# Two dense tiles' gates: one-hot products against additions in memory by indirect transfers

## The reference, cut to what matters

```python
def peer(xn, w_q, sub_keys, u, v):
    q = (xt @ w_q).reshape(t, PEER_HEADS, 2, PEER_HALF)
    sc = jnp.einsum("thpc,hpnc->thpn", q, sub_keys)
    top_s, top_i = lax.top_k(sc, PEER_TOPK)              # 16 of 128, for each half
    cand_s = ...; cand_i = ...                           # 256 pairs of a head
    best_s, best_pos = lax.top_k(cand_s, PEER_TOPK)      # 16 of them
    idx = jnp.take_along_axis(cand_i, best_pos, axis=-1) # expert = 128 * left + right
    gate = jax.nn.softmax(best_s, axis=-1)
    # for each token: sum over its 8 * 16 slots
    hid = gelu(x . u[idx]) * gate
    out = sum(hid * v[idx])
```

## Time and profile before

| | before |
|---|---|
| median of 3 runs | 2321.95 us |
| the profiled execution: span | 2321.5 us |
| PE busy | 2190.6 us (94%) |
| DVE busy | 1544.2 us (67%) |
| ACT busy | 864.4 us (37%) |
| POOL busy | 438.8 us (19%) |
| memory read and written | 404.6 and 44.8 MB |

### The profile page before, as it was taken

The page is one execution under the profiler, slowest core; times in us unless marked ns, Lnnn a source line. Parts: engine busy times, 40 slices in busy tenths (PEclk is TensorE's granted clock), DMA queues, the critical chain, the costliest instruction groups (busy, mean ns, idle before and its releaser), DMA issues. The chain is left out here.

```text
span 2321.5 us, 29188 instructions
## 1 busy us (share of the span) xinstructions
PE 2190.6 (94%) x11110; PEld 1895.1 (82%) x11110; DVE 1544.2 (67%) x2711; ACT 864.4 (37%) x1431; POOL 438.8 (19%) x307
## 2 busy tenths in 40 slices
PE   7999899899999899898999999999998999988898
PEld 6777788688999889888788888999996798876577
DVE  4545434325999989864888888688887624447734
ACT  3345323322334644863333333333334432222322
POOL 0100000000122010001434335266661000004200
PEclk9999999899999999999999999999998999998999
DMA  5321133211678674678999999799992322310220
GB/s 213 111 87 55 50 142 132 95 37 60 227 251 258 184 245 156 195 233 284 358 384 385 383 384 367 255 356 358 357 335 108 146 85 93 107 55 1 109 100 37
DMA packets 211836, 451.35 MB, mean 194 GB/s; under 512 B 13808, under 2 KB 133616, under 8 KB 204912
## 3 DMA queue, kind: packets, MB, share of 16 engines
q1 hardware_dynamic: 174832, 315.24, 39.7%
q0 software_dynamic: 36864, 134.23, 15.9%
HBM read 404.60 MB, written 44.83 MB: 194 GB/s over the span
## 5 line engine op out<-in xcount | busy, mean ns | idle before, releaser
L1604 PE MATMUL bank<-Vh,Hh 128*128 128x512 f32 x768 | 299.7, 390 | 4.7 <-DVE Hl L1687 4.6
L1606 PE MATMUL bank<-Vh,Hl 128*128 128x512 f32 x768 | 300.3, 391 | 0.0
L1605 PE MATMUL bank<-Vl,Hh 128*128 128x512 f32 x768 | 300.1, 391 | 0.0
L1626 ACT ACTIVATE Vh<-Vr 128x1024 fp32r<-128x1024 f32 x128 | 135.8, 1061 | 302.4 <-PE bank L1606 296.6
L934 PE MATMUL bank<-XH,Ue 128*128 128x384 f32 x672 | 232.2, 346 | 13.8 <-DVE Ue L923 13.8
L972 POOL DMA_INDIRECT ring<-in_v,gidx x128 | 205.8, 1608 | 164.7 <-DVE x_res L984 69.1
L935 PE MATMUL bank<-XL,Ue 128*128 128x384 f32 x672 | 227.3, 338 | 0.0
L936 PE MATMUL bank<-XH,Ue 128*128 128x384 f32 x672 | 227.2, 338 | 0.0
L1682 DVE TENSOR_TENSOR Vl<-Vr,Vh 128x1024 fp32r<-128x1024 f32 x128 | 156.3, 1221 | 49.6 <-ACT Vh L1626 46.7
L972 POOL DMA_INDIRECT ring<-in_u_rows,gidx x92 | 114.8, 1248 | 381.6 <-DVE ghid L977 206.2
L1604 PEld LDWEIGHTS bank<-Vh,Hh 128*128 128x128 f32 x768 | 144.6, 188 | 35.6 <-DVE Hl L1687 6.4
(11 more groups left out here) (386 smaller groups left out, 4935.3 us busy)
## 6 DMA issues: line engine op xcount, KB each, us to landing
Vr<-in_v SPq DMA_DIRECT2D x128, 512.0 KB
ur<-in_u SPq DMA_DIRECT2D x86, 512.0 KB
W<-in_w_stream SPq DMA_DIRECT2D x19, 2048.0 KB, 8.2
Gr<-gates SPq DMA_DIRECT2D x32, 768.0 KB
XT<-in_u SPq DMA_DIRECT2D x42, 512.0 KB
early<-ar SPq DMA_DIRECT2D x84, 192.0 KB
A<-early SPq DMA_DIRECT2D x84, 192.0 KB
xs<-in_w_mixer SPq DMA_DIRECT2D x14, 1024.0 KB
```

What stands on the lines that cost most here:

```text
L1604: pe.matmul(ps, Hh[r][:, tok], Vh[r][:, cut], start=p == 0, stop=False)
L1605: pe.matmul(ps, Hh[r][:, tok], Vl[r][:, cut], start=False, stop=False)
L1606: mm = pe.matmul(ps, Hl[r][:, tok], Vh[r][:, cut], start=False, stop=p == PK - 1)
L1626: act.activation(Vh[q % RV][:], Vr[q % RR][:], ACT.Copy).then_inc(v_hi, 1)
```

## The change

- `phase_merge`: GpSimd clears a tile `zeros` [128, 512], and SP stores it over the first two dense tiles' part of the table in memory (`Scattered.clear`: eight stores of 2 MB, ahead of the phase's other loads); SP waits for them at the phase's end.
- `phase_table`: after `choose(1)` and `choose(2)` DVE computes each slot's place in the table (six small instructions), and `gates` writes to `sca.gate`. For each of the two tiles and each of the 128 slots GpSimd issues one indirect DMA that adds the 128 tokens' gates, one element each, to their places in memory (`Scattered.put`). Every 16 slots (one head) it waits until all before have landed, since two heads can name the same place. GpSimd first issues 15 of the gathers; the other 15 stand at every fifth put.
- The slices, turns and stores of those two tiles go. The third tile's carry 8 early blocks. The order is choose 0, 1, 2, 3, 7 blocks (`E_MID`), slices, 26 blocks (`E_LAST`); `choose` has 14, 19, 19 and 19 blocks and 0, 10, 10 and 10 dots. 112 blocks are early, 16 late.
- `phase_experts`: SP also waits for the last puts before the first load of the table. Positions 0 to 7 and 120 to 127 are late.
- Some semaphores of the second layer are merged, to have enough.

```diff
-E_SCORE, E_SLICES, E_LAST = (14, 18, 18, 18), 4, 4
-EARLY = sum(E_SCORE) + DT * E_SLICES + E_LAST
+SCATTERED = 2
+E_SCORE, E_MID, E_SLICES, E_LAST = (14, 19, 19, 19), 7, 8, 26
+EARLY = sum(E_SCORE) + E_MID + (DT - SCATTERED) * E_SLICES + E_LAST
-DOTS = (0, 12, 12, 12)
+DOTS = (0, 10, 10, 10)
...
@@ phase_merge, SP and POOL
             sp.dma_start(gat.x[:], c.t["norm2"]).then_inc(c.const_in, 16)
+            sca.clear(sp, zeros)
...
+            sp.wait_ge(sca.zeroed, 16 * 4 * SCATTERED)
...
+            pool.memset(zeros[:], 0.0).then_inc(sca.cleared, 1)
             norm_rsqrt(pool, c, N_EXPERTS)
...
+class Scattered:
+    ZERO = 512
...
+    def clear(self, sp, zeros):
+        sp.wait_ge(self.cleared, 1)
+        for quarter in range(4 * SCATTERED):
+            flat = self.c.t["gates"][quarter].rearrange("a p b t -> (a p b t)").rearrange("(p r w) -> p r w", p=P, w=self.ZERO)
+            sp.dma_start(flat, zeros[:].unsqueeze(1).broadcast_to(list(flat.shape))).then_inc(self.zeroed, 16)
+
+    def put(self, pool, n, s):
+        if s == 0 and n == 0:
+            pool.wait_ge(self.zeroed, 16 * 4 * SCATTERED)
+        if s % TOPK == 0 and s > 0:
+            pool.wait_ge(self.landed[n], 16 * s)
+        cells = self.c.t["gates"].rearrange("q a p b (t o) -> (q a p b t) o", o=1)
+        at = bass.IndirectOffsetOnAxis(ap=self.place[:, n, s:s + 1], axis=0)
+        pool.indirect_dma_start(out=cells, out_offset=at, in_=self.gate[:, n, s:s + 1], in_offset=None,
+                                compute_op=ALU.add).then_inc(self.landed[n], 16)
+
+    def done(self, eng):
+        for n in range(SCATTERED):
+            eng.wait_ge(self.landed[n], 16 * SLOTS)
...
@@ phase_table, POOL
-            for s in range(DOTS_TABLE):
-                gat.fetch(pool, s)
+            dots = 0
+            while dots < DOTS[1] + RG:
+                gat.fetch(pool, dots)
+                dots += 1
+            for n in range(SCATTERED):
+                pool.wait_ge(chosen, n + 2)
+                for s in range(SLOTS):
+                    if s % BETWEEN == BETWEEN - 1 and dots < DOTS_TABLE:
+                        gat.fetch(pool, dots)
+                        dots += 1
+                    sca.put(pool, n, s)
...
@@ phase_table, PE
-            products(E0, E_SCORE[0] + E_SCORE[1] + LEAD)
-            turn(1)
-            products(E2 + LEAD, E_SCORE[2] - LEAD)
-            slices(0, EH0)
-            products(E3, E_SCORE[3])
-            slices(1, EH1)
-            slices(2, EH2)
+            products(E0, EM + LEAD)
+            turn(3)
+            products(EM + LEAD, E_MID - LEAD)
+            slices(2, EH[2])
             products(EL, E_LAST)
...
@@ phase_table, DVE, choose(n)
+                if n <= SCATTERED:
+                    row = float(PK * Q_TOK)
+                    link(dve.tensor_copy(part[:, 0], out3[:, 0]))
+                    link(one(1, part[:, 0], Q_BLK - 1, ALU.bitwise_and))
+                    dve.tensor_copy(abf[:, 1], part[:, 1])
+                    link(dve.tensor_scalar(abf[:, 0], out3[:, 0], row, c.tab[:, T_PLACE + tt:T_PLACE + tt + 1], ALU.mult, ALU.add))
+                    link(dve.scalar_tensor_tensor(out=abf[:, 0], in0=abf[:, 1], scalar=Q_TOK - row, in1=abf[:, 0], op0=ALU.mult, op1=ALU.add))
+                    link(dve.scalar_tensor_tensor(out=sca.place[:, n - 1], in0=out3[:, 1], scalar=float(Q_BLK * Q_TOK), in1=abf[:, 0],
+                                                  op0=ALU.mult, op1=ALU.add))
                 gates(n)
...
@@ phase_experts, SP
                     early.table_done(sp)
+                    sca.done(sp)
                     load_g(0)
```

More of the change, by code:

```diff
@@ L113 @@
 T_PICK = T_SIN + TT * DH
-NTAB = T_PICK + TT * SH
+T_PLACE = T_PICK + TT * SH
+NTAB = T_PLACE + SCATTERED
 R_GQK = 0
@@ L985, in add, with __init__ @@
                                  op0=ALU.mult, op1=ALU.add).then_inc(self.used, 1)
+class Scattered:
+    ZERO = 512
+    def __init__(self, c, ctx):
+        self.c = c
+        own = c.rows[:, R_GQK:R_GQK + 2 * SCATTERED * SLOTS].rearrange("p (f n s) -> p f n s", f=2, s=SLOTS)
+        self.place, self.gate = own[:, 0].bitcast(U32), own[:, 1]
+        self.cleared, self.zeroed = signals(c.nc, ctx, "sc_cleared sc_zeroed")
+        self.landed = signals(c.nc, ctx, " ".join(f"sc_landed{i}" for i in range(SCATTERED)))
+    def clear(self, sp, zeros):
[15 more added lines that the diff above has]
+            eng.wait_ge(self.landed[n], 16 * SLOTS)
 def phase_query(c, SC, early):
@@ L1086, in _, with phase_table @@
                         query_out(dve, dve.tensor_copy, g, qd)
-def phase_table(c, ijg, early, SC, gat):
+def phase_table(c, ijg, early, SC, gat, sca):
     nc, t = c.nc, c.t
@@ L1144, in phase_table @@
         E0, E1, E2 = 0, E_SCORE[0], E_SCORE[0] + E_SCORE[1]
[L1145 to L1149, removed]
+        E3 = E2 + E_SCORE[2]
+        EM = E3 + E_SCORE[3]
+        EH = [EM + E_MID + max(tt - SCATTERED, 0) * E_SLICES for tt in range(DT)]
+        EL = EH[DT - 1] + E_SLICES
+        J0 = SCATTERED * NSL
+        PER = E_SLICES // 4
         TICKS = [*[0.2] * NQ, *[0.52] * NQ, *[0.2] * NQ, *[0.28] * NQ, 0.43, 1.07, *[0.15] * PH, *[0.42] * PH, *[0.15] * PH, *[0.21] * PH,
@@ L1188, in stores @@
                 for i in range(4):
-                    early.load(sp, e + i + 3)
+                    turns(e + i * PER, PER - 1)
+                    early.load(sp, e + i * PER + PER + 2)
                     store(4 * tt + i)
[L1191 to L1197, removed]
+                    early.keep(sp, e + i * PER + PER - 1)
+            turns(E0, EM + E_MID)
+            for tt in range(SCATTERED, DT):
+                stores(tt, EH[tt])
             turns(EL, E_LAST)
@@ L1278, in slices @@
                     quarter = j // QSL
-                    if s % QSL == 0 and quarter >= 2:
-                        act.wait_ge(early.tabled[quarter % 2], 16 * PIECES * (quarter // 2))
+                    if s % QSL == 0 and quarter - 4 * SCATTERED >= 2:
+                        act.wait_ge(early.tabled[quarter % 2], 16 * PIECES * (quarter // 2 - 2 * SCATTERED))
                     if s + 1 < NSL:
@@ L1303, in _ @@
             scored(1, E1)
[L1304 to L1307, removed]
+            scored(2, E2)
             scored(3, E3)
-            slices(1, EH1)
-            slices(2, EH2)
+            gelus(EM, LEAD)
+            turned(3)
+            gelus(EM + LEAD, E_MID - LEAD)
+            slices(2, EH[2])
             gelus(EL, E_LAST)
@@ L1480, in _, with phase_experts @@
             choose(2, E2)
-            fill(0, EH0 + 1)
-            slices(0, EH0)
             choose(3, E3)
-            fill(0, EH1 + 1)
-            slices(1, EH1)
-            slices(2, EH2)
+            fill(0, EH[2] + 1)
+            slices(2, EH[2])
             fill(0, EARLY)
-def phase_experts(c, early, gat):
+def phase_experts(c, early, gat, sca):
     nc, t = c.nc, c.t
@@ L2544, in build @@
                 if upto >= 5:
-                    phase_table(c, ijg, early, SC, gat)
+                    phase_table(c, ijg, early, SC, gat, sca)
             if upto >= 6:
-                phase_experts(c, early, gat)
+                phase_experts(c, early, gat, sca)
         with ExitStack() as mix:
@@ L2585, in _tables @@
                     tab[(2 * (SG * cc + g) + x) * HG + h, T_PICK + (SG * cc + g) * HG + h] = 1.0
+    for tt in range(SCATTERED):
+        tok = tt * P + np.arange(P)
+        tab[:, T_PLACE + tt] = tok // Q_TOK * (PK * PK * Q_TOK) + tok % Q_TOK
     nf = DH // 4
```

67 lines of the change are left out of this document (35 added, 32 removed).

## The result

The changed kernel takes 2502.45 us, the median of 4 runs (2499.35 to 2505.7), beside 2323.05 us for the kernel before (4 runs, 2321.37 to 2325.95). The ratio is 1.0766, with a 95% interval of 1.0749 to 1.0784: 7.7% slower. The forecast was 2356 us in a range of 2275 to 2405, so the side was right and the size was not; the time lies next to the 2520 us of the rival "the add costs an extra descriptor".

A forecast was written before the change was run, and what follows sets the result against it. GpSimd's queue of puts was to bound the table stage and transfers the expert loop: +100.4 (table) - 68 (loop) + 2 (PE's clock) = +34, so 2321.95 + 34 = 2356 us, range 2275 to 2405.

The forecast's parts named there:

- the add costs an extra descriptor: Rival, table stage: two reads set up per element, 0.93 us more per put, end near 1315, about 2520 us; chance 0.11.
- The price of a put: GpSimd in the table stage: priced like an indirect gather, 0.94 us, 1.24 us from start to start undisturbed.
- The puts' surroundings: Table stage: first put at 699, 2.1 us each during slices, 3 us per wait for 16 landings, end at 1147.
- GpSimd keeps pace: Rival, table stage: puts at an undisturbed 1.24 us, end at 1083, 2290 us; break-even 1.38 us per put; chance 0.27.
- Cheaper puts: Rival, table stage: a 4-byte put needs less than a 4 KB gather, PE's 1072 ends the stage, 2279 us; chance 0.10.
- No ceiling: Rival, expert stage: slow puts, but DMA reaches 440 GB/s, loop 580 us, 104 less, 2320 us in all; chance 0.12.
- The 518 us: PE's part of the table stage: 466 for 112 blocks, 31 for slices, some 21 filling and stalls, to 1072 us.
- the sentence in brackets: Table stage: VectorE uses a dot each 8 us, five rows ahead; last dot up to 5 us late, cost nothing.
- 61 and 3 to enter: Third tile's slices with 8 blocks, bounded by PE: 61 us and 3 to enter, 64, of which 33 are blocks.
- Zeros: Eight 2.1 MB stores before `phase_merge`'s loads take 37 and 43 us; cost taken as nothing, range 0 to 18 us.
- The expert loop: Expert stage: transfers at 405 GB/s, 4.49 us per position, loop 618 us, 68 us less; between 104 and 49.
- The clock: PE after standing still before the expert stage: 2 us added for its clock.

The follow-up runs named there:

- e1_plain: The changed kernel with its 256 one-element puts as plain writes, without the addition: 2370.04 us.
- e2_back: The changed kernel with each put turned into a gather of single elements from memory, without addition, two tiles' gates left out: 2370.16 us.
- e7_half_loads: The changed kernel loading only half of each early block and of the table after the expert stage's first positions, all compute instructions kept: 2450.67 us.
- e5_between3: The changed kernel with a gather at every third put instead of every fifth: 2502.71 us.
- e6_one: The changed kernel with one tile scattered, 88 early blocks, 12 dots per choosing, a gather every third put: 2298.89 us, ratio 0.9894 to the kernel before.
- e3_one_tile_put: The changed kernel without the second tile's 128 puts, that tile's gates left out: 2338.57 us.
- e9_slices8: The kernel before with 8 early blocks in all three tiles' slices, 92 early blocks, nothing scattered: 2314.36 us, ratio 0.9955.
- e4_early112: The kernel before with 112 early blocks instead of 84, all slices kept, nothing scattered: 2382.66 us, ratio 1.025.

## Why the prediction was right or wrong

*The price of a put: the step that failed.* The sum took the put as a gather, since the gather was the nearest row, and left the dearer add to a rival at 0.11. Measured: 1.55 us undisturbed, 1.86 from start to start, against the 0.94 and 1.24 taken; the mean is 1.71 + 0.30. e1_plain puts the price of the addition at 0.53 us in the mean, 135 us for the 256. The stage's other terms were 11 us too high together, and so its end accounts for 124 of the 146 us by which the forecast was short. The rival named the addition, with 0.93 us per put and an end near 1315; measured are 0.58 undisturbed and 1271, and its mechanism, two reads set up for each element, no run shows. That its 2520 us lie so near is in part luck: it put the too large 0.93 on top of the undisturbed case (about 1083 + 238), and on top of the forecast's own 1147 it would have ended at 1385. Its sentence "Nothing in the trace speaks for or against it" was true, and should have told against 0.11: the trace had one price near an add's (a gather's) and nothing that held it from above, and a queue with 256 equal instructions multiplies such an error by 256. The range's upper end of 2405 left that open side out.

*The puts' surroundings: sized well.* Without the addition the stage ended at 1135.9 against 1147 (e1_plain). The first put started at 699.03, forecast for 699. The waits for 16 landings were 29.4 us for 14, 2.1 us each, where 3 were taken. The puts in the slices took 1.84 us in the mean, and so did those before them, against 1.55 once VectorE was idle (83 puts after 1102 us, mean 1551 ns). Since PE and ScalarE stand still then too, these means don't say whose work it is; the timelines, put by put, do. The 113 puts of the kernel after beside which VectorE runs neither a `TENSOR_TENSOR` nor a dot, both instructions with two inputs, all take 1.55 to 1.57 us, 30 of them before 1101 us, while PE still has products; the 143 beside one take 1.84 in the mean and up to 2.66. Why a put is longer beside them no run shows.

*The rivals.* "GpSimd keeps pace" had its break-even at 1.38 us per put; at 1.18 + 0.30 even the plain put of e1_plain is above it, and that kernel is slower than before, as the rule of the forecast says. "Cheaper puts" is out by e2_back: a single element costs GpSimd what 4 KB do. Both rivals also leaned on PE's end at 1072 or 1083 us, and with the cheap transfers of e1_plain and e2_back the last early Gelu stood at 1102.4 and 1100.5. "No ceiling" is out by e7_half_loads.

*PE's part of the stage.* The 518 us came out where the rows were in time: 1069.5 in e5_between3 against 1072. (The "29 us or so" that the prediction has left over in the old stage are 22 by its own 56.9 us per tile of slices; the sum took 21.) The step that failed in the kernel after is the sentence in brackets: VectorE's dots were to be late by "up to 5 us, cost taken as nothing", and PE lost 32 us to them (1101.97). With a put at 1.86 us, five puts and a gather take over 10 us, more than VectorE's 8 us per dot, so every dot after the five rows ahead is late. The price of a put is not all of it: in e1_plain, with puts of 0.97 us, VectorE waits for no row between 780 and 900 us, and the last early Gelu is at 1102.39 all the same. There ScalarE waits 83.1 us before its early Gelus, between 554 and 1100, for a releaser that the profile calls only "remote", where no such wait stands in the kernel after; what it is stays open. PE's late end costs nothing while GpSimd's queue is later still. The slices' tile took from 926.4 to 987.8, 61.4 us, against 61 and 3 to enter; its eight blocks come 7.73 us apart, one for two slices, so 3.87 per slice where 3.81 were reckoned. The place instructions and the lost cover in `choose` show nowhere.

*Zeros: nothing, as forecast.* PE's last product of the line of `phase_merge` that reads these loads starts at 380.2 us, and at 380.4 before. The eight stores landed 18.9 us after their issue in the median.

*The expert loop: the mechanism right, the size at the range's edge.* Taken were 405 GB/s and 68 us; measured were 388 GB/s [as in rows 6] and 47.3 us, and the lower bound named in the prediction was 388 and 49. I had chosen a value between the plateau that a window of 20 us showed and a peak of four microseconds, although the loop is 640 us long. That is 21 of the 146 us. VectorE's round with two adds takes 1708.95 - 1704.48 = 4.47 us, so it is close behind. Of the windows of 20 us in the loops here, with or without the change, the highest had 399 (e6_one, 1580 to 1600 us; 397 in the kernel after); the 407 of the earlier trace rows was a window of four.

*The clock.* The 2 us for PE's start after standing still were an estimate from no row, and they don't show in the sum: from the first gather to the first accumulating product it is 35.3 us, where it was 37.3. The granted clock was low there: 0.50 from 1274 to 1278 us with PE busy throughout and 15 products, where the kernel before has 0.81 and 21 products from 1050 to 1054. So something else in that stretch is shorter by more, and which part isn't shown.

*What stays open.* The 4 us by which the rest after the loop is longer (556.1 against 552.0) came back in e1_plain, e2_back, e3_one_tile_put, e5_between3, e6_one and e9_slices8, whose edits differ, by half in e4_early112 (554.3), and not in e7_half_loads (552.4). It is small beside the 12 us by which runs of the kernel before differ; I don't know its cause. And I don't know which work GpSimd does in the added 0.58 us.

The whole: 224 - 2 - 47 + 4 = 179 us of span, against 100 + 2 - 68 = 34 forecast.

## What to carry to other kernels

An indirect transfer that adds takes GpSimd 1.55 us where the plain one takes 0.97, and a queue with hundreds of them is priced by its pitch: before moving work to the engine that is least busy, multiply the pitch, with an upper bound for each form that no row shows, and compare it with the slack of that stage. Moving work out of a stage pays only down to that stage's next limit: here 28 blocks cost 113 us where they went and gave 58 back, since with them moved the transfers are the limit at some 388 GB/s; take the ceiling from the longest window, not from the best one. A dose that ends with the engine beside it (one tile, 128 puts, both done by 1022 us) gained 1.1%, a third of it or more by fuller slices that need no put, where the double dose lost 7.7%.

## What the runs showed of the hardware that I had not expected

- The addition turns a put of 128 single elements from 32 packets into 144, and costs GpSimd 0.58 us more (1.55 against 0.97 us).
- A gather of 128 single elements of 4 bytes takes GpSimd as long as one of 128 rows of 4 KB: 0.94 us.
- VectorE's instructions with two inputs (`TENSOR_TENSOR` and the dots) lengthen a put beside them: 1.84 us in the mean for 143 puts, against 1.55 to 1.57 for each of the other 113.
- Where the DMA engines' share is 1.02 or more in the expert loop, they move 380 to 393 GB/s in the windows of 20 and 100 us printed above, whether a position needs 1.62 or 1.82 MB; the highest window of 20 us in the loops had 399.
